# Two-block transformer kernel on one Trainium2 core: the experts' rows added to the residual by TensorE in turned form, and two norm scales applied after the projections

## What is computed

```
r   = h + w0 * y0 + w1 * y1                  # two expert rows per token, weights w0, w1
h2  = r * rsqrt(mean(r*r) + eps) * final_g   # end of the first block: the new residual
u   = h2 * rsqrt(mean(h2*h2) + eps) * norm_mix[0]
proj = u @ w_in                              # q, f, i, g of the recurrence (HGRN2)
f = low + span * sigmoid(f); q = silu(q); g = silu(g); i is taken as it is
```

## Time and profile before

| | us |
|---|---|
| median of three runs | 2353.63 |
| the profiled execution's own time | 2358.84 |
| its span in the trace | 2357.0 |
| TensorE busy, share of the span | 88% |
| mean granted TensorE clock | 0.957 |

### The profile page before, as it was taken

How to read it: one execution, slowest core, us unless ns; L and a number is a source line. 1 busy time by engine, 2 the same in 40 slices (tenths; PEclk the granted TensorE clock), 3 DMA queues, 4 the chain that set the end, 5 groups by cost and what they waited for, 6 DMA issues and landing times.

```text
span 2357.0 us, 25197 instructions
## 1 busy us (share of the span) xinstructions
PE 2080.2 (88%) x9900; PEld 1510.4 (64%) x9900; DVE 937.3 (40%) x1125; ACT 669.2 (28%) x835; POOL 352.8 (15%) x349
## 2 busy tenths in 40 slices
PE   6997756877777773999989999999999999999997
PEld 5884532332223221788877888887788987888876
DVE  5428640000000004567765432444775334332333
ACT  3433220000000002666744221223222423221222
POOL 0000002000000000355551110011343201100100
PEclk9997777999999997999999999999999999999999
DMA  5220145999999993211122222223222322222220
GB/s 200 90 90 1 51 193 216 422 421 422 421 421 420 421 420 146 72 63 64 57 76 72 90 106 90 90 91 123 76 86 90 138 77 90 90 95 101 89 90 36
DMA packets 57636, 377.51 MB, mean 160 GB/s; under 512 B 8944, under 2 KB 9040, under 8 KB 14032
## 3 DMA queue, kind: packets, MB, share of 16 engines
q1 hardware_dynamic: 50544, 358.83, 38.8%
q0 software_dynamic: 7008, 17.50, 2.0%
HBM read 370.46 MB, written 15.26 MB: 164 GB/s over the span
## 4 chain that ended last, share of the span: by engine, by line
PE 69%; DMA 18%; DVE 7%; issue 3%; ACT 2%; POOL 1%; SPq 0%; DVEq 0%; POOLq 0%; ACTq 0%
PE bank L529 19%; PE bank L530 19%; PE bank L531 19%; DMA moe_w<-weights_in 17%; PE bank L748 2%; PE bank L725 2%; PE bank L887 2%; PE bank L899 1%; POOL k_rot L2398 1%; DVE w_lo L1586 1%; PE bank L1095 1%; DVE tile L1703 1%; DVE o_tmp L2030 0%; DVE tile L1714 0%; DVE tile L1710 0%
## 5 line engine op out<-in xcount | busy, mean ns | idle before, releaser
L529 PE MATMUL bank<-u_hi,w_hi 128*128 128x512 f32 x1216 | 489.0, 402 | 7.6 <-DVE u_lo L1910 6.4
L530 PE MATMUL bank<-u_lo,w_hi 128*128 128x512 f32 x1216 | 481.3, 396 | 0.0
L531 PE MATMUL bank<-u_hi,w_lo 128*128 128x512 f32 x1216 | 481.0, 396 | 0.0
L1586 DVE TENSOR_TENSOR w_lo<-raw,w_hi 128x2048 fp32r<-128x2048 f32 x96 | 234.1, 2439 | 292.8 <-ACT w_hi L1154 292.6
L725 PE MATMUL bank<-moe_w,xe 128*64 128x512 f32 x1088 | 263.3, 632 | 87.7 <-DMA moe_w<-weights_in 86.5
L529 PEld LDWEIGHTS bank<-u_hi,w_hi 128*128 128x128 f32 x1216 | 228.6, 188 | 66.4 <-issue 10.8
L531 PEld LDWEIGHTS bank<-u_hi,w_lo 128*128 128x128 f32 x1216 | 228.5, 188 | 55.9
L530 PEld LDWEIGHTS bank<-u_lo,w_hi 128*128 128x128 f32 x1216 | 228.9, 188 | 55.2 <-issue 2.2
L1154 ACT ACTIVATE w_hi<-raw 128x2048 fp32r<-128x2048 f32 x96 | 183.6, 1912 | 272.1 <-PE bank L531 271.4
L725 PEld LDWEIGHTS bank<-moe_w,xe 128*64 128x64 f32 x1088 | 91.6, 145 | 258.5 <-issue 258.4
L529 PE MATMUL bank<-w_hi,u_hi 128*128 128x256 f32 (+1 forms) x512 | 155.3, 303 | 12.5 <-DVE u_lo L1721 6.8
(11 more groups left out here) (395 smaller groups left out, 2645.5 us busy)
## 6 DMA issues: line engine op xcount, KB each, us to landing
moe_w<-weights_in SPq DMA_DIRECT2D x204, 1024.0 KB, 25.1
raw<-weights_in SPq DMA_DIRECT2D x128, 1024.0 KB, 4.8
y_pairs<-pair_rows POOLq DMA_DIRECT2D x4, 1024.0 KB, 8.2
res<-x_in SPq DMA_DIRECT2D x1, 2048.0 KB, 7.7
token_rows<-xn POOLq DMA_DIRECT2D x1, 2048.0 KB, 7.9
v_rows<-vals SPq DMA_DIRECT2D x2, 1024.0 KB
vals<-v_rows SPq DMA_DIRECT2D x2, 1024.0 KB, 7.5
out<-out_tile SPq DMA_DIRECT2D x4, 512.0 KB, 2.6
```

What stands on the lines that cost most here:

```text
L529: nc.tensor.matmul(out_ap, a_hi, b_hi, start=first, stop=False)
L530: nc.tensor.matmul(out_ap, a_hi, b_lo, start=False, stop=False)
L531: return nc.tensor.matmul(out_ap, a_lo, b_hi, start=False, stop=last)
L1586: nc.vector.tensor_tensor(w_lo[:, n % 2], raw[:, n % RAW], w_hi[:, n % 2].bitcast(F32), ALU.subtract) \
```

## The change

What it does, part by part.

1. **Turned sum on PE.** The transposes of `xn` go. While the last rows are stored, PE multiplies each 128 x 128 block of `res` with the identity (32 float32 matmuls, start of a group in each of the eight banks). When a block of `y_pairs` has landed, it multiplies its 2 x 8 pieces with diagonal matrices that hold the tokens' weights (`share_diag`, made before the experts by DVE), 64 float32 matmuls in all, into the same banks.
2. **Scales later.** `u_hi`, `u_lo` are made from the banks with `mix_gain = final_g * norm_mix[0]` alone; the tokens' scale goes on behind the projections: on DVE for f, q and g (`normalize`, two per unit, 24 in all), on ACT as a scale for i. `hs` gets its scale from POOL (eight multiplications), for the next residual.
3. **Norm beside.** DVE still sums rows (`row_sum`), ACT squares them, DVE sums squares with `final_g` squared (`row_squares`), and both scales are worked out for the four token columns, made into diagonals and spread by two matmuls with ones (`spread_late`) between the halves of unit j = 1.
4. **Transfers.** `y_pairs` is loaded by SP, `over_slots` ahead of the first gather instead of behind the last scatter, the parameters for the bounds of f before the experts.
5. **Order in p = 0.** The splits of the first units and the f work move behind; f is made in j = 2 there.

The diff, cut to its core:

```diff
@@ SP, behind the loads of the first four units of the mixer
+            sp.wait_ge(pairs_stored, PAIRS_STORED)
+            for b in range(TB):
+                sp.dma_start(y_pairs[b][:], pair_rows[2 * P * b:2 * P * (b + 1)].rearrange("(p k) d -> p k d", k=2)) \
+                    .then_inc(y_landed[b], 16)
@@ PE, behind the experts
-            pe.wait_ge(xn_ready, 2 * TB)
-            for c in range(KC):
...
-                for b in range(TB):
-                    mm = nc.tensor.transpose(bank[c % 4][:, b * P:b * P + P], xn[:, b, c * P:c * P + P], ident)
-                mm.then_inc(h_turned, 1)
+            for c in (0, 1, 2, 3, 4, 7, 5, 6):
+                if c == 5:
+                    pe.wait_ge(y_left, ROUNDS)
+                if c == 6:
+                    pe.wait_ge(y_right, ROUNDS)
                 for b in range(TB):
+                    nc.tensor.matmul(of_block(c, b), res[:, b, c * P:c * P + P], ident, start=b == 0, stop=False)
+            for b in range(TB):
+                pe.wait_ge(y_landed[b], AFTER_MOE + 16)
+                for c in range(KC):
+                    for k in range(2):
+                        mm = nc.tensor.matmul(of_block(c, b), y_pairs[b][:, k, c * P:c * P + P], share_diag[:, k, b],
+                                              start=False,
+                                              stop=b == TB - 1 and k == 1)
+                    if b == TB - 1:
+                        mm.then_inc(h_turned, 1)
-            norm(0)
+            def spread_late():
+
+                pe.wait_ge(hs_out, HS_OUT + KC)
+                for n in range(2):
+                    pe.wait_ge(diag_ready, DIAG_READY + n + 1)
+                    nc.tensor.matmul(bank[6 + n][:], ones, late_diag[n][:].rearrange("p b t -> p (b t)"), start=True, stop=True) \
+                        .then_inc(n_sum, 1)
@@ PE, in the loop over p and j
                     for half in range(2):
+                        if p == 0 and j < 2:
+                            pe.wait_ge(hs_out, HS_OUT + 2 * j + half + 1)
...
+                        if (p, j, half) == (0, 1, 0):
+                            spread_late()
@@ ACT
+            for b in range(TB - 1):
+                row_square(b)
+            for c in range(3):
+                high(c)
+            act.wait_ge(res2_ready, TB)
+            residual(0)
+            for c in range(3, KC):
+                high(c)
+            row_square(TB - 1)
+            residual(1)
+            split(U_HG + 1)
+            for c in range(2, KC):
+                residual(c)
             act.wait_ge(rms_arg, 4)
+            nc.scalar.activation(late[:, 4:6], late[:, 2:4], ACT.Sqrt).then_inc(root_ready, 1)
+            split(U_HG + 2)
+            for n in range(2):
+                act.wait_ge(n_sum, n + 1)
+                nc.scalar.activation(late_row[n][:], bank[6 + n][:], ACT.Copy).then_inc(late_ready, 1)
@@ DVE
+            for c in range(KC):
+                dve.wait_ge(u_hi_ready, 2 * KC + c + 1)
+                nc.vector.scalar_tensor_tensor(u_lo[:, c], bank[c][:], mix_gain[:, c:c + 1], u_hi[:, c].bitcast(F32),
+                                               ALU.mult, ALU.subtract).then_inc(u_lo_ready, 1)
...
+            row_squares(0)
+            row_squares(1)
+            split(U_HG + 1)
+            row_squares(2)
+            chain(row_squares(3))
...
+            for n in range(2):
+                nc.vector.tensor_tensor(late_diag[n][:], ident.unsqueeze(1).to_broadcast([P, TB, P]),
+                                        late[:, 7 - n].unsqueeze(2).to_broadcast([P, TB, P]), ALU.mult).then_inc(diag_ready, 1)
+            split(U_HG + 2)
+            def normalize(p, j, tile):
+
+                for half in range(2):
+                    if half == 0:
+                        dve.wait_ge(proj_ready, 4 * p + j + 1)
+                    else:
+                        dve.wait_ge(unit_used, U_HG + 4 * p + j + 1)
+                    nc.vector.tensor_tensor(tile[:, half], bank[(2 * j + half) % 4][:], late_row[0][:], ALU.mult) \
+                        .then_inc(pre_ready, 1)
...
                     recurrent_work(beat + 2)
+                    if j == 0 and p:
+                        normalize(p, 0, run[s])
+                    if j == 1:
+                        if p == 0:
+                            dve.wait_ge(late_ready, LATE_READY + 1)
+                            normalize(0, 0, run[s])
+                        normalize(p, 1, qry[s])
+                    if j == 3:
+                        normalize(p, 3, o_raw[:, 2 * p:2 * p + 2])
                     recurrent_work(beat + 3)
@@ POOL
             pool.wait_ge(slots_landed, 48)
+            pool.dma_start(over_slots[0:CAP], slot_table[MAIN + P:].rearrange("(v s) c -> s v c", s=CAP)).then_inc(slots_landed, 16)
...
+            nc.gpsimd.memset(y_mark[:], 0).then_inc(pairs_stored, 1)
...
+            pool.wait_ge(late_ready, LATE_READY + 2)
+            for c in range(KC):
+                nc.gpsimd.tensor_tensor(hs[:, c], hs[:, c], late_row[1][:], ALU.mult).then_inc(h0_ready, 1)
```

More of the change, by code:

```diff
@@ L225, in build @@
         over_slots = tiny("over_slots", [N_OVER, 2], I32)
-        y_pairs = place("y_pairs", [TB, 2, D], at_a)
+        y_pairs = [place(f"y_pairs{b}", [2, D], at_b + 20 * KB2 if b == 3 else at_a + 4 * b * KB2) for b in range(TB)]
         MAIN = P * NPAIR
@@ L246, in build @@
         rms = place("rms", [T], at_a2 + 2 * KB2)
-        u_tmp = [place(f"u_tmp{n}", [T], at_a2 + (3 + n) * KB2) for n in range(3)]
+        row_sum = place("row_sum", [TB, D], at_b)
+        row_sq = [place(f"row_sq{b}", [D], at_b + at * KB2) for b, at in enumerate((8, 10, 16, 18))]
+        late = place("late", [8, TB], at_x + 192)
+        late_diag = [place(f"late_diag{n}", [TB, P], at_b + at * KB2) for n, at in enumerate((12, 24))]
+        late_row = [place(f"late_row{n}", [T], at_b + at * KB2) for n, at in enumerate((14, 13))]
+        share_diag = place("share_diag", [2, TB, P], at_b + 26 * KB2)
         o_hi = place("o_hi", [HH, T], at_b, F32R)
@@ L1346, in root @@
             def root(k):
[L1348 to L1358 removed]
+                act.wait_ge(n_sum, 2 + k)
+                nc.scalar.activation(rms[:], bank[4][:], ACT.Sqrt, scale=1.0 / D, bias=eps).then_inc(n_root, 1)
             def split_trip(n, i, per):
@@ L1431, in _ @@
                     recurrent_work(beat + 2)
[L1432 to L1446 removed]
+                    if j == (0 if p else 1):
+                        for half in range(2):
+                            act.wait_ge(pre_ready, PRE_READY + 6 * p + half + 1)
+                            nc.scalar.activation(run[s][:, half], run[s][:, half], ACT.Sigmoid).then_inc(f_sig, 1)
@@ new lines, in _ @@
+                    if j == 1:
+                        for half in range(2):
+                            act.wait_ge(pre_ready, PRE_READY + 6 * p + half + 3)
+                            nc.scalar.activation(qry[s][:, half], qry[s][:, half], ACT.Silu).then_inc(q_taken, 1)
+                    if j == 2:
+                        for half in range(2):
+                            if half == 0:
+                                act.wait_ge(proj_ready, 4 * p + j + 1)
+                            else:
+                                act.wait_ge(unit_used, n + 1)
+                            for b in range(2):
+                                c = slice(b * 256, b * 256 + 256)
+                                last = nc.scalar.activation(val[s][:, 2 * half + b], bank[half][:, c], ACT.Copy,
+                                                            scale=late[:, 7, 2 * half + b:2 * half + b + 1])
+                            last.then_inc(v_taken, 1)
@@ L1447, in _ @@
+                    if j == 3:
+                        for half in range(2):
+                            act.wait_ge(pre_ready, PRE_READY + 6 * p + half + 5)
+                            nc.scalar.activation(o_raw[:, 2 * p + half], o_raw[:, 2 * p + half], ACT.Silu).then_inc(g_taken, 1)
                     recurrent_work(beat + 3)
@@ L1888, in _ @@
                                                ALU.mult, ALU.add).then_inc(res2_ready, 1)
-            dve.wait_ge(sq_ready, 4 * TB)
-            nc.vector.tensor_scalar(rms2[:, 5], rms2[:, 4], 1.0 / D, EPS, ALU.mult, ALU.add).then_inc(rms_arg, 1)
-            dve.wait_ge(root_ready, 4)
-            chain(nc.vector.reciprocal(rms2[:, 7], rms2[:, 6]))
-            for b in range(TB):
-                nc.vector.tensor_scalar(xn[:, b], res[:, b], rms2[:, 7, b:b + 1], None, ALU.mult).then_inc(xn_ready, 1)
@@ new lines, in row_squares @@
+            def row_squares(b):
+                dve.wait_ge(sq_ready, 3 * TB + b + 1)
+                return nc.vector.scalar_tensor_tensor(row_sq[b][:], row_sq[b][:], 1.0, fg_row, ALU.mult, ALU.mult,
+                                                      accum_out=late[:, 1, b:b + 1])
+            row_squares(0)
[3 more added lines that the diff above has]
+            chain(row_squares(3))
```

(1 more changed line is left out.)

200 lines of the change are left out of this document (86 added, 114 removed).

## The result

The changed kernel takes **2342.89 us**, the median of six runs (2341.63 to 2347.20). The kernel before has a median of 2358.09 in six runs (2353.54 to 2362.63): the three shown before and three more, which were slower (2358.76 to 2362.63). The ratio is 0.9941, with a 95% interval of 0.9925 to 0.9956: 15 us faster. The profiled execution took 2342.92 against the 2339.5 forecast for it.

A forecast was written before the change was run, and what follows sets the result against it. PE, busy 88% of the span, was taken to bound the kernel, except where it waits. 26.4 - 1.7 - 1.5 - 1.5 - 1.0 - 1.4 = 19.3 us gained: 2339.5 profiled, 2334.3 median, range 2328 to 2343.

The forecast's parts named there:

- The seam: Between experts and mixer, 892.0 to 954.3: first half unit ends at 927.9 instead of 954.3, 26.4 us gained.
- Rows: First pair rows (y_pairs) land at 905.4 instead of 909.2, the last block at 912.9.
- sum: PE's 64 products of the pair rows take 16.8 us, done at 922.2.
- clock: PE's granted clock is down when its sum starts at 905.4 and back 5.1 us later, costing 2.6 us.
- hidden chain of the scales: Row sums, squares and roots run beside PE's products, with cover until 939.1; second diagonal ready at about 938.
- signs of being wrong: PE waiting over 4 us for far_q or diagonals, k_dec waits every unit, y_pairs at 909 or later, gather over 3 us later.
- Spread: Two float32 matmuls of 512 columns, alone on PE, 0.86 us each: 1.7 us lost.
- First gather: over_slots, issued before the first gather, delays it: 1.5 us lost, between 1.0 and 3.3.
- p = 1 to 3: DVE's normalizes ahead of the next keys make these late at six places by 0.1 to 0.3: 1.0 us lost, 0 to 3.
- p = 0: f made in j = 2, far sides ready only 0.5 us ahead, POOL multiplying meanwhile: 1.5 us lost, between 0 and 6.
- second rival: POOL's multiplications block DVE in p = 0 (f operations, split): 6 us beyond the slack, time 2338.8; chance 0.17.
- The end: From 1203 PE waits for DVE's keys, so two normalizes in j = 3 of p = 3 lose 1.4 us, 0 to 3.

The follow-up runs named there:

- e6_warm: Changed kernel with 24 overwritten products of the residual with the identity put ahead of the real ones, so PE does not stand before rows land: 2339.40 us.
- e7_slots_back: Changed kernel with the load of over_slots put back behind the last scatter, as in the kernel before: 2349.97 us.
- e5_no_norm: Changed kernel without DVE's normalizing in p = 1 to 3; ACT reads the banks directly, the tokens' scale left out there: 2340.45 us.
- c5_first_only: Changed kernel with the edits of e1_hs_later and e6_warm, and the first head's reciprocal and product (beats 22, 38, 54) one beat later: 2336.76 us, ratio 0.9911.
- e1_hs_later: Changed kernel with POOL's eight multiplications of hs moved from before its first gaps into beats 16 to 23, one each: 2339.21 us.
- e2_f_early: Changed kernel with DVE's f work of p = 0 put between the two halves of q's normalizing in j = 1: 2341.48 us.
- e4_norm_after_beat: Changed kernel with the normalizes of p = 1 to 3 (DVE) and ACT's activations that take them placed behind the fourth beat's work: 2351.30 us.
- c6_changed_again: The changed kernel unaltered, run once more on the chip of c5_first_only: 2345.62 us, ratio 0.9948.

## Why the prediction was right or wrong

**The seam: right.** 26.4 us were forecast at the end of the first half unit. Measured: 954.3 - 928.38 + 1.03 = 27.0. Rows, sum, clock and the hidden chain of the scales came as drawn; e6_warm shows the clock's part as 2.3 for 2.6, e7_slots_back the part of `over_slots`, 3.3. None of the signs of being wrong showed as they were put: the wait for `far_q` was 2.8, not over 4.

**Spread: right.** 27.0 less the 25.4 at j = 2 is 1.6, for 1.7.

**First gather: mis-sized.** 0.5 to 0.7 for 1.5. The lower end was the send of an indirect transfer of 1.05; the send of this plain one is 0.54. The experts' end came 1.0 later, of which this is a part; the rest is within what executions differ by there.

**p = 1 to 3: the step that failed by most.** 1.0 was taken, with 3 as the upper end; 5.0 were lost: 3.4 from "p = 1" to "p = 3" and 1.6 in the rest of p = 3. The cause was right (with no normalizes nothing is lost, e5_no_norm), and so was one of the places (keys behind the normalizes, where the reciprocal stands); the size was not. I counted six places of 0.1 to 0.3. There are more in each p: 0.4 at the keys of j = 1, 0.6 at the head output four beats later, which no step had, and 0.4 in all at j = 3, 1.7 per p with small ones. How the lateness gets from the keys to the head output, through DVE's split and far sides, is read from the timelines; c5_first_only bears it out, where moving the reciprocal away from the normalizes of j = 1 takes the whole 1.2 out of p = 2.

**p = 0: the other step that failed.** The sum took 1.5 and measured 4.7. The schedule held DVE's f operations at two microseconds (947.3 to 949.3), as if POOL's multiplications beside them had no effect, and the 1.5 put on for them was not worked out. The working, 1.3 for each operation, stood in the second rival, with a chance of 0.17. That rival named the cause (e1_hs_later), but not the size: it had a wait of up to 6, the four operations were 3.5 longer, and the wait was 2.8. Its split was not hit, since POOL was done by then. The other 1.7 are the clock behind the wait (e6_warm), which no step had. That its total of 6 for p = 0 comes near 4.7 is in part luck.

**The end: right, and a term that was missing.** 1.2 are lost at 1204, for 1.4 forecast, and none without normalizes (e5_no_norm). The sum has nothing for the clock of this stage, which gives back 1.3, because it fell twice in the kernel before's execution and at neither place in this one. "From p = 3 to the output" measures 1.5, which looks like the 1.4; it is 1.6 + 1.2 - 1.3, and the agreement is luck.

**From the profiled execution to the median: the other half of the miss.** Of the 8.6 us between 2334.3 and 2342.89, 3.4 are the steps above (2342.92 against 2339.5; 4.5 at the output, of which 1.2 come back behind 1800). The other 5.2 are the difference that I carried over from the three runs shown before: their median lay 5.2 below the profiled execution. Over six runs it lay 0.75 below. Three runs that range over 4 us, of a kernel whose runs range over 9, did not carry this correction. Against the median of its own six runs the kernel gained 15.2, for 19.3 forecast.

**Sum.** Forecast: 26.4 - 1.7 - 1.5 - 1.5 - 1.0 - 1.4 = 19.3. Measured up to the output: 27.0 - 1.6 - 4.7 - 5.0 - 1.2 + 1.3 = 15.8, and 14.8 with the 1.0 by which the experts ended later, of which the gather is 0.5 to 0.7.

## What to carry to other kernels

Work that leaves the critical path is not free if it lands beside another engine's: eight POOL multiplications that nobody waited for cost 3.7 us, because DVE's short operations from SBUF stretched beside them (0.43 us to 1.41), in a place without slack. When operations are added to a queue that is "busy 158 of 234", price them at the places where the queue is already late (a 3.3 us reciprocal just ahead) and follow the lateness on until it runs out; a share of busy time says nothing of this. When two executions are compared, look at the granted clock of both: a gain can be the other kernel's low clock (1.3 us here). And a difference between a profiled execution and a median of three runs is a draw, to be put into the range and not into the forecast.

## What the runs showed of the hardware that was not expected

A wait of PE can cost more than its length: behind the same wait of 2.8 us for the far sides the granted clock fell to 0.50 for 3.4 us in six traces (the changed kernel, twice, e2_f_early, e4_norm_after_beat, e5_no_norm and e7_slots_back), which cost 1.7, and did not fall in e6_warm. The six also had the low clock earlier in the seam (from 902 to 905 us on), and e6_warm had not; whether that decides it was not tried. In the last stage the clock was low for anything from 0 (e2_f_early, e6_warm and c6_changed_again) to 13.6 us (e7_slots_back). Low clock there costs what PE has to do in it: the changed kernel's 3.4 us from 1190.6 on cost nothing (c6_changed_again, the same kernel without them, loses the same 2.8 to 1204 and gets the same 1.3 back), and the kernel before's two falls cost it 1.3.
